# A two-block, float32 network on one Trainium2 core: layer stages reordered on two PSUM banks, attention steps stretched over three parts, late modulation on TensorE, and both feed-forward norms applied after the matmuls

## The reference, cut to what matters

```
# a layer of the first block, l = 0, 1
mod = silu(c) @ w_ada[l] + b_ada[l];  shift, scale, gate = split(mod, 3)
h = rms_norm(x, norm_g[l]) * (1 + scale) + shift
gq, gk, gv, glr, gz, dq, dk, dv, dz = split_columns(h @ w_in[l])
# gq, gk, gv: a causal conv of 4 taps, silu, then gated linear attention in chunks of 64,
#   o_gla = rms_norm(o, gla_norm_g) * silu(gz)
# dq, dk, dv: two softmaxes per head over 4 heads, blocks of 128 queries, chunk-causal mask,
#   q, k = rms_norm(q), rms_norm(k);  attn = softmax(q0 k0) - lam * softmax(q1 k1)
#   o_diff = rms_norm(attn @ v, diff_norm_g) * (1 - lam_init) * silu(dz)
x = x + gate * (concat(o_gla, o_diff) @ w_out[l])
# a feed-forward network
x = x + 0.5 * (silu(g) * u) @ w_out,   g, u = split(rmsnorm(x, gain) @ w_in)
```

## Time and profile before

| | us |
|---|---|
| median of 3 runs | 1945.54 (1943.96 to 1948.92) |
| the profiled execution: its own time | 1945.24 |
| its span | 1943.5 |
| TensorE busy | 1798.3 (93% of the span) |
| VectorE, ScalarE, GpSimd busy | 949.8, 635.0, 663.2 |

### The profile page before, as it was taken

One profiled execution on the slowest core, in us unless ns is written; L12 is line 12 of the kernel. 1 busy time (PEld: TensorE's weight loads), 2 busy tenths in 40 slices (PEclk: granted clock), 3 DMA queues, 4 the chain that ended last, 5 costly groups with the idle time before them and its releaser, 6 DMA issues.

```text
span 1943.5 us, 22498 instructions
## 1 busy us (share of the span) xinstructions
PE 1798.3 (93%) x8960; PEld 1500.5 (77%) x8960; DVE 949.8 (49%) x917; ACT 635.0 (33%) x779; POOL 663.2 (34%) x163
## 2 busy tenths in 40 slices
PE   5979987989987789999999899989999989999997
PEld 2868866768976668888888798868888868888886
DVE  4895357565547574545322333674322555454323
ACT  3331344244245333333323322223222243333221
POOL 2231111224221033434344334323434324343342
PEclk9988888989988889999999899999999989999998
DMA  8472111112111022232223232312222312222222
GB/s 319 172 267 82 44 44 44 65 44 87 66 66 44 22 87 87 86 108 86 81 91 109 84 112 86 108 49 103 86 108 86 107 67 87 107 86 94 89 89 73
DMA packets 30914, 180.98 MB, mean 93 GB/s; under 512 B 4466, under 2 KB 4596, under 8 KB 14340
## 3 DMA queue, kind: packets, MB, share of 16 engines
q1 hardware_dynamic: 24480, 161.50, 23.3%
q10 hardware_dynamic: 6372, 18.62, 2.7%
HBM read 178.00 MB, written 2.10 MB: 93 GB/s over the span
## 4 chain that ended last, share of the span: by engine, by line
PE 61%; issue 31%; POOL 4%; DVE 2%; ACT 0%; POOLq 0%; DVEq 0%; ACTq 0%
PE ps L812 20%; PE ps L814 19%; PE ps L813 19%; POOL wl L463 4%; PE ps L843 1%; PE ps L842 1%; PE ps L841 1%; PE ps L918 0%; DVE xl L1250 0%; DVE cv L1650 0%; PE ps L879 0%; DVE y L1287 0%; PE ps L882 0%; PE ps L881 0%; DVE tmp L1659 0%
## 5 line engine op out<-in xcount | busy, mean ns | idle before, releaser
L463 POOL TENSOR_TENSOR wl<-raw,wh 128x2048 fp32r<-128x2048 f32 (+1 forms) x152 | 661.2, 4350 | 1254.3 <-ACT wh L506 1254.2
L812 PE MATMUL ps<-xh,wh 128*128 128x512 f32 x1408 | 559.0, 397 | 41.9 <-DVE xl L1480 15.3
L813 PE MATMUL ps<-xl,wh 128*128 128x512 f32 x1408 | 555.6, 395 | 0.0
L814 PE MATMUL ps<-xh,wl 128*128 128x512 f32 x1408 | 554.5, 394 | 0.0
L506 ACT ACTIVATE wh<-raw 128x2048 fp32r<-128x2048 f32 x152 | 291.2, 1916 | 601.1 <-PE ps L814 530.2
L812 PEld LDWEIGHTS ps<-xh,wh 128*128 128x128 f32 x1408 | 268.9, 191 | 106.9 <-issue 33.5
L814 PEld LDWEIGHTS ps<-xh,wl 128*128 128x128 f32 x1408 | 269.0, 191 | 57.4
L813 PEld LDWEIGHTS ps<-xl,wh 128*128 128x128 f32 x1408 | 269.4, 191 | 55.6
L1614 DVE TENSOR_TENSOR fl<-tmp,fh 128x512 f32 x44 | 194.9, 4430 | 80.9 <-ACT fh L724 80.9
L841 PE MATMUL ps<-wh,xh 128*128 128x256 f32 x608 | 184.3, 303 | 0.0
L842 PE MATMUL ps<-wh,xl 128*128 128x256 f32 x608 | 178.0, 293 | 0.0
(11 more groups left out here) (226 smaller groups left out, 1879.0 us busy)
## 6 DMA issues: line engine op xcount, KB each, us to landing
raw<-ffn_in_stream SPq DMA_DIRECT2D x44, 1024.0 KB, 4.8
raw<-mixer_stream SPq DMA_DIRECT2D x40, 1024.0 KB, 4.8
raw<-layer_stream SPq DMA_DIRECT2D x36, 1024.0 KB, 4.8
raw<-ffn_out_stream SPq DMA_DIRECT2D x32, 704.0 KB, 4.1
ada_late<-w_ada ACTq DMA_DIRECT2D x32, 512.0 KB, 5.2
ada_w<-w_ada SPq DMA_DIRECT2D x8, 1024.0 KB, 18.7
x<-x_t SPq DMA_DIRECT2D x1, 2048.0 KB, 7.8
y_t<-y SPq DMA_DIRECT2D x8, 256.0 KB, 2.2
```

What stands on the lines that cost most here:

```text
L463: nc.gpsimd.tensor_tensor(wl[u][:, 0:size], raw[u][:, 0:size], wh[u][:, 0:size].bitcast(F32), ALU.subtract).then_inc(w_ready, 1)
L812: nc.tensor.matmul(bank_ap, w0, x0, start=first, stop=False)
L813: nc.tensor.matmul(bank_ap, w0, x1, start=False, stop=False)
L814: return nc.tensor.matmul(bank_ap, w1, x0, start=False, stop=last)
```

## The change

The projections of a layer use banks 0 and 1 only: a unit's tile t goes to bank t, and a part that begins tile t waits until ScalarE has emptied tile t of the unit just before. k is projected before q (parts 16 to 23 are k, 24 to 31 q). The attention steps run from the largest block of queries to the smallest, step s after part 35 + s, with `turn(s - 2)`, `pv(s - 3)`, `score(s)` on TensorE, and two pairs of banks for the scores (2, 3 and 4, 5). The second softmax stays in PSUM, and the division by the first row sum moves to `copy_o`. The output gains move from the gating to the splits of the mix (`mix_h`, `mix_l`); the gating is cut in `gated_r` and `gated_z`; o_gla is turned between parts 53 and 55, and o_diff between the four halves of the first output units. The late modulation is 16 tiles of 4 matmuls on TensorE (`late_tile`, the same form as L898), out of 3 buffers of 1 MB. Both ffn norms are late: the unnormed `x * gain` is split inside the residual loop before (`raw_high`, `raw_low`), the ffn starts on it, `r_bc` is the spread reciprocal root, and it multiplies the gate half before silu and the output tiles in the residual. The norm before layer 1, before the mixer and at the end stay as they were.

```diff
-             (("conv", L_CONV), ("q", L_Q), ("k", L_K), ("v", L_V), ("z", L_Z))
+             (("conv", L_CONV), ("k", L_K), ("q", L_Q), ("v", L_V), ("z", L_Z))
...
-    put(36, "turn_keys")
-    for s in range(STEPS + 2):
-        put(38 + s, "attn", s)
...
+    for s in range(STEPS + 3):
+        put(35 + s, "attn", s)
+        if s >= 6 and s % 4 == 2:
+            put(36 + s, "diff_ss", 3 - (s - 6) // 4)
...
+    put(51, "z_act", 0)
+    for tb in range(TB):
+        put(52, "gated_z", 0, tb)
+        put(53 + tb // 2, "mix", tb)
+    put(54, "diff_root")
+    put(54, "z_act", 1)
...
+        for piece in range(ADA_LATE):
+            if n == 4 + piece * 8 // 5:
+                order.append(("ada", piece))
... in part(), TensorE
+                    if half == 0:
+                        pe.wait_ge(banks_free[(unit - 1) % 2], emptied(unit - 1, t))
                     if p == 0:
-                        pe.wait_ge(banks_free[u], emptied(unit, 1) - 2)
                         pe.wait_ge(w_ready, unit + 1)
... TensorE
+            def late_tile(n):
+                pe.wait_ge(late_landed[buf], 16 * sum(loads))
+                for b in range(ADA_COLS):
+                    last = nc.tensor.matmul(ps[32 * b:32 * b + 32, 2], c_wide[:, k],
+                                            ada_late[buf][:, b * S:b * S + S], start=(k == 0), stop=(k == KT - 1))
+                last.then_inc(late_used, 1)
... the attention stage on TensorE
-                        if s < STEPS:
-                            score(s)
-                        if 1 <= s <= STEPS:
-                            turn(s - 1)
-                        if s >= 2:
-                            pv(s - 2)
+                        if 2 <= s < STEPS + 2:
+                            turn(s - 2)
+                        if s >= 3:
+                            pv(s - 3)
+                        if s < STEPS:
+                            score(s)
... after the table, TensorE
+                pe.wait_ge(mix_low, l * 8 + TB)
+                for u in range(2):
+                    claim(0, out_unit, u)
+                    chunk_ready(0, out_unit, u)
+                first_out(0, 0, gla)
+                first_out(0, 1, gla)
+                turn_output(4)
+                turn_output(5)
+                first_out(1, 0, gla)
...
+            def raw_high(n, gain, m):
+                act.wait_ge(x_ready, (n - 1) * KT + m + 1)
+                nc.scalar.activation(xh[:, m], x[:, m], ACT.Copy, scale=gain[:, m:m + 1]).then_inc(high_ready, 1)
+            def raw_low(n, gain, m):
+                dve.wait_ge(high_ready, SPLIT0[f"norm{n}"] + m + 1)
+                nc.vector.scalar_tensor_tensor(out=xl[:, m], in0=x[:, m], scalar=gain[:, m:m + 1],
+                                               in1=xh[:, m].bitcast(F32), op0=ALU.mult, op1=ALU.subtract)
... the ffn loop, VectorE
+                        if late:
+                            dve.wait_ge(tile_done, i * 4 + (2 * unit + 2 * u + 1))
+                            nc.vector.tensor_tensor(gate[:, u], ps[:, 2 * u], r_bc[:], ALU.mult)
... residual after an ffn, VectorE
+                    if late:
+                        y_in = gate[:, m % 2]
+                        link(nc.vector.tensor_tensor(y_in, ps[:, 2 * u + t], r_bc[:], ALU.mult))
```

More of the change, by code:

```diff
@@ L802, in _ @@
             chunk += M_MERGE
-            output_squares(4, unit, chunk, M_OUT)
-            ffn("ffn2", 4)
+            output_squares(4, unit, chunk, M_OUT, gains[:, 2])
+            ffn("ffn2", 4, True)
             norm(5, splits=False)
@@ L1046, in _ @@
                         part(*at_)
+                    elif stage == "ada":
+                        if l == 0:
+                            late_tile(at_[0])
+                    elif stage == "ada_turn":
+                        if l == 0:
+                            pe.wait_ge(late_rows, at_[0] + 1)
+                            if at_[0]:
+                                pe.wait_ge(late_mod, at_[0])
+                            for i in range(TB):
+                                last = nc.tensor.transpose(ps[:, 3, i * P:i * P + P], sumsq[:, i * P:i * P + P],
+                                                           ident[:])
+                            last.then_inc(late_cols, 1)
                     elif stage == "lr":
@@ L1158, in ffn @@
[L1158 to L1159 removed]
+                        out_unit_of(i, u)
+            def ffn(name, n, late):
                 unit, chunk = UNIT0[name], CHUNK0[name]
[L1161 removed]
+                if late:
+                    first_feature_unit(unit, chunk, (xh, xl), SPLIT0[f"norm{n}"], n)
+                    norm_spread(n)
+                else:
+                    norm(n)
+                    first_feature_unit(unit, chunk, (xh, xl), SPLIT0[f"norm{n}"])
@@ L1551, in _ @@
[L1551 to L1565 removed]
+                        j = at_[0]
@@ L1616, in ffn @@
                                                 ).then_inc(low_ready, 1)
-                residual(n + 1, unit + FT, lambda m: 0.5, True)
-            ffn("ffn1", 2, gains[:, 0])
+                residual(n + 1, unit + FT, lambda m: 0.5, True, late)
+            ffn("ffn1", 2, gains[:, 0], True)
             norm(3, gains[:, 1])
@@ L1691, in _ @@
             unit += M_MERGE
-            residual(4, unit, lambda m: 1.0, False)
-            ffn("ffn2", 4, gains[:, 2])
+            residual(4, unit, lambda m: 1.0, False, gain=gains[:, 2])
+            ffn("ffn2", 4, gains[:, 2], True)
             norm(5, gains[:, 3])
```

527 lines of the change are left out of this document (294 added, 233 removed).

## The result

The changed kernel takes 1889.18 us (median of 4 runs, 1887.43 to 1889.57) against 1947.23 of before on the same chip; the ratio is 0.971, 95% interval 0.9693 to 0.9726. The forecast was 1863, with 1848 to 1882 as the range of its own case and 1843 to 1895 with rivals 1 to 3: the direction holds, the time lies outside the own range and inside the wide one, and of the 82.2 us forecast only 58 came.

What follows compares the result with a forecast made beforehand. The prediction took large matmuls (0.2284 us each, TensorE never idle) as the floor, with losses in the layers and ffn starts. 2 x (-25.7 - 3.8 + 1.3) - 13.1 - 12.7 = -82.2 from 1945.2 gave 1863 us, range 1843 to 1895.

Steps and rivals of the forecast that it cites:

- its own case: Whole kernel: the summed gains come out at 1863 us, own range 1848 to 1882; chance 0.64.
- rivals 1: Attention, both layers: split passes still hold VectorE, half of the loss stays, +28 us, 1891; chance 0.18.
- 2: Layer 0's late modulation tiles: each waits 2 us for its load, +28 us, 1891; chance 0.08.
- Rival 3: End of a layer: `take_high` is not late after all, -8 us per layer, 1847; chance 0.06.
- Attention: Attention in each layer: 27.7 us lost, 2 us left with the longer chain, so -25.7 us.
- The cause is one place: Attention's lost time: GpSimd's 4.56 us split of a weight chunk holds a VectorE instruction on two columns for 4.43 us.
- End of a layer: Each layer's end: 12.3 of 16.1 us lost stays, including TensorE standing 8.3 us for both chunks; -3.8 us.
- Two banks: Layer projections: late emptying by ScalarE makes TensorE stand at part 10; +1.3 us per layer.
- Rival 4: Layer projections: ScalarE empties two banks late at most units, the clock falls and the kernel is slower; chance 0.03.
- Layer 0 only: Layer 0: multiply-adds -21.6, column sums -13.7, late tiles +17.0, turns +0.7, load waits +4.5; sum -13.1 us.
- ffn starts: Both ffn starts: TensorE keeps its stream, -14.2 us; later residual work +1.5, sum -12.7 us.
- the strided load: Output gains' load in 512 pieces of 4 bytes, before layer 0's first unit: counted as nothing, at most 3 us.

Runs made afterwards that it cites:

- out_start: Changed kernel, with TensorE starting a layer's output projection at the first chunk and awaiting the second only before the second unit's products: 1869.47 us, ratio 0.9598.
- short_first: Changed kernel with attention's chain one part shorter and rows in the order of before, 128 key columns first: 1907.66 us, ratio 0.9807.
- early_norms: Changed kernel with both ffn norms finished ahead of the first ffn matmul again, as before the change: 1903.51 us, ratio 0.978.
- Shift_before: Kernel before the change with its arena moved up by 32 bytes and nothing else: 1955.41 us, ratio 1.0051.
- same_place: Changed kernel with its arena at the same address as before the change, 122816 in place of 121824: 1879.74 us, ratio 0.9646.
- align_after: Changed kernel with its arena beginning at a multiple of 64 bytes: 1884.67 us, ratio 0.9686.

## Why the prediction was right, and what it missed

*The range.* The direction was reasoned and came out; that the time fell inside the range was luck in part. The sum's own range ended at 1882. What reached to 1895 was the price of rivals 1 and 2, at 1891 each, and neither came: attention lost 4 us a layer to its forecast and not 12, and the tiles waited once. The measured time lies near 1891 for two reasons that no case had. Rival 1 was also priced too high: half of 27.7 us in place of the 2 already in the sum is 11.85 a layer, +24 and 1887, not +28. Rival 3 did not come (the wait was there), and out_start shows what it would have been worth.

*Attention.* The sum had -25.7 a layer for the whole loss less 2 us; measured in layer 1 was 19.4 and the 1.8 of transposes, 21.2, and in layer 0 20.1 and 1.8, 21.9. The direction and the place were right, the term mis-sized by 4.5 and 3.8 us. Part of it is seen: the waits left are 3.1 us where I had 2, and the product with v costs 0.17 us more in some 12 steps, 2 us, which I had counted at nothing. The working named the wrong main cause: "With one part between score and transpose there is no room for that" covers 7 to 8 of 21 us. In short_first, still with that one part, 10 to 11 us of the loss are already gone. "The cause is one place" was read from 19.0 us of waits of which 6.9 were the scores', for the exponentials, with one pair of banks; the sum had no term for the second pair.

*End of a layer.* The forecast wait of 8.3 us was 8.64, and the wait for the next chunk stood at 1.17 for 1.3. -3.8 was right to about a microsecond (5.05 less the 1.8 of moved transposes, 3.25). Read as a forecast it was good; as advice it was poor, since it took both `chunk_ready` ahead of the first output matmul for given. Lifting one of them until its products are due gave 17 us.

*Two banks.* One wait of 1.1 us at part 10 of layer 1 and none in layer 0, where the sum had 1.3 in each. Rival 4 did not come.

*Layer 0 only.* Layer 0 is longer than layer 1 by 17 us now, by 32.5 before. The 16 tiles took 0.99 to 1.00 us each (1.06 forecast), and the loads were waited for once, 2.3 us in place of 4.5. Rival 2 did not come.

*ffn starts.* 14.3 us by early_norms' median, 13.1 by its span; forecast 12.7. The wait of 1.5 for `wl` was 1.75. That the table shows only -9.0 comes from the next point, 2.33 in each ffn.

*The first thing the prediction missed* stands in no term: "nothing in the change shortens a large matmul", but it lengthened 1056 of them in the ffns, 576 in the mixer and 384 in the layers' outputs. Shift_before and same_place undo and redo it: 9.4 us each by the medians, 7.2 of it seen in the stretches in both; the layers' outputs add 2.3, since their mix tiles lie in the arena only since the change (96 matmuls in 22.45 us, 21.87 before). The diff showed the cause, `o_g` smaller and `c_wide` new ahead of the arena, and I did not ask what lies behind them.

*The second* was put too low: the strided load, "I count nothing, since TensorE then waits for the modulation weights, and at most 3 us". It cost 5.2. The load was hidden, but ScalarE's next issue was not, and the first norm's root stood behind it in the same program order.

These two make 14.7 of the 24.4 us (5.2, 7.2 and 2.3) between forecast and trace, attention some 8; the rest is 1.3 at the norm between the layers and some 2 in the mixer at half clock behind the gating unit, against 2.2 saved on the tiles' loads. The last two are read from one execution.

## What to carry to other kernels

Before costing a change at nothing, look at what it moves in memory and on the queues: a buffer that shrinks moves all that lie behind it, and here a load in 4-byte pieces was paid by the next issue of its queue (9.11 us against 2.23). Where an engine waits for several things at once ahead of a block of work, ask which of them its first piece needs. When several edits act on one stretch, undo them one by one before naming the cause: here the one that the argument rested on gave about a third, and about half was not taken apart.

## What the runs showed of the hardware that I had not expected

A large matmul's pace depends on where its moving tile lies in 256 bytes, against its weights: 227.5 ns at the same place, 229.6 when 64 bytes above, 233.3 to 234.2 at the six other steps of 32, whatever the bank and with no other engine at work. By these figures a kernel made of such matmuls would lose up to 2.9%, an estimate. It was measured in one execution of each of two kernels, with 128x128 weights and 512 columns of four bytes alone; the Trainium skill, SBUF — State Buffer, "Operand start alignment", speaks of which addresses are allowed and says that its runs timed nothing.

An issue of a load behind one of 512 pieces of 4 bytes took 9.11 us in the changed kernel and 8.86 in align_after, against 2.23 behind the same 2 KB in 128 pieces.
